# Token-major projections 512 columns wide, over two half slabs of weight rows, with four sums open

## The reference

```
h  = rms_norm(x);  p = h @ w_in            # q_a k_a v_a o_a i f q_b k_b v_b g_a g_b
y_a = sigmoid(o_a) * norm(mLSTM(silu(conv(q_a, k_a)), v_a, i, f))     # 8 heads
y_b = stick_breaking(norm(q_b), norm(k_b), v_b)                        # 8 heads
x  = x + (sigmoid(g_a) * y_a + sigmoid(g_b) * y_b) @ w_out
x  = x + square(relu(rms_norm(x) @ w_up)) @ w_down                     # 1024 -> 4096 -> 1024
h  = rms_norm(x);  p = h @ nsa_w_in        # q, 3 pairs of k and v, gates, z (3 x 1024)
o  = compressed, selected and window attention, 16 heads
y  = (sum over the three branches of gate * o * silu(z)) @ nsa_w_out
out = x + rms_norm(y)
```

## Time and profile before

| | |
|---|---|
| median of 3 runs | 1437.09 us |
| the profiled execution | 1437.17 us, its span 1435.4 us |
| mean granted TensorE clock | 0.994 of full speed |
| TensorE matmuls | busy 1393.7 us, 97% of the span |
| VectorE, ScalarE, GpSimd | busy 679.2, 612.0 and 173.8 us |
| DMA | 120.5 MB, mean 84 GB/s |

### The profile page before, as it was taken

One profiled execution on the slowest core, in us unless ns is written; L12 is line 12 of the kernel. 1 busy time (PEld: TensorE's weight loads), 2 busy tenths in 40 slices (PEclk: granted clock), 3 DMA queues, 4 the chain that ended last, 5 costly groups with the idle time before them and its releaser, 6 DMA issues.

```text
span 1435.4 us, 21763 instructions
## 1 busy us (share of the span) xinstructions
PE 1393.7 (97%) x9021; PEld 1219.5 (85%) x9021; DVE 679.2 (47%) x1152; ACT 612.0 (43%) x989; POOL 173.8 (12%) x243
## 2 busy tenths in 40 slices
PE   6999999999999999999999999999999999999998
PEld 4898777786777889899898998988899999898998
DVE  5653443553333453543434334341146777776654
ACT  4245444515555433421413214144424666665332
POOL 1001232001111000000000000000901333231000
PEclk9999999999999999999999999999999999999999
DMA  8655434343333333133222332244341322222221
GB/s 175 102 104 84 70 76 60 60 59 59 48 51 52 74 101 89 60 109 97 88 88 88 100 105 88 88 135 147 101 90 38 91 73 67 68 92 64 85 77 60
DMA packets 110559, 120.50 MB, mean 84 GB/s; under 512 B 5231, under 2 KB 106719, under 8 KB 110480
## 3 DMA queue, kind: packets, MB, share of 16 engines
q1 hardware_dynamic: 106960, 108.70, 31.4%
q0 software_dynamic: 3376, 10.38, 3.0%
q10 hardware_dynamic: 144, 0.31, 0.1%
HBM read 116.55 MB, written 2.82 MB: 83 GB/s over the span
## 4 chain that ended last, share of the span: by engine, by line
PE 87%; DVE 5%; ACT 2%; DMA 2%; issue 1%; POOL 1%; SPq 0%; DVEq 0%
PE ps_g L514 69%; PE ps_z L1107 2%; PE ps_z L1144 2%; PE ps_t L1179 2%; DMA w_raw<-in_w_in 2%; PE ps_z L985 1%; PE ps_z L973 1%; PE ps_t L961 1%; PE ps_t L908 1%; DVE w_lo L487 1%; PE ps_t L1029 1%; DVE probs L1653 1%; PE ps_z L896 1%; DMA tile_t<-bias_rev_dram 1%; PE ps_t L280 1%
## 5 line engine op out<-in xcount | busy, mean ns | idle before, releaser
L514 PE MATMUL ps_g<-act_hi,w_hi 128*128 128x512 f32 x784 | 309.8, 395 | 6.6 <-DVE act_lo L599 4.1
L487 DVE TENSOR_TENSOR w_lo<-w_raw,w_hi 128x2048 fp32r<-128x2048 f32 (+1 forms) x96 | 220.3, 2295 | 198.0 <-ACT w_hi L479 197.9
L514 PE MATMUL ps_g<-act_hi,w_lo 128*128 128x512 f32 x784 | 306.3, 391 | 0.0
L514 PE MATMUL ps_g<-act_lo,w_hi 128*128 128x512 f32 x784 | 305.9, 390 | 0.0
L479 ACT ACTIVATE w_hi<-w_raw 128x2048 fp32r<-128x2048 f32 (+1 forms) x96 | 182.0, 1896 | 178.0 <-PE ps_g L514 167.9
L514 PE MATMUL ps_g<-w_hi,act_hi 128*128 128x256 f32 x832 | 240.8, 289 | 1.4 <-DVE act_lo L597 0.7
L514 PE MATMUL ps_g<-w_lo,act_hi 128*128 128x256 f32 x832 | 235.1, 283 | 0.0
L514 PE MATMUL ps_g<-w_hi,act_lo 128*128 128x256 f32 x832 | 235.0, 282 | 0.0
L514 PEld LDWEIGHTS ps_g<-act_hi,w_hi 128*128 128x128 f32 x784 | 147.7, 188 | 39.4 <-DVE w_lo L487 4.5
L514 PEld LDWEIGHTS ps_g<-act_hi,w_lo 128*128 128x128 f32 x784 | 147.5, 188 | 31.5
L514 PEld LDWEIGHTS ps_g<-act_lo,w_hi 128*128 128x128 f32 x784 | 147.8, 188 | 29.7
(11 more groups left out here) (291 smaller groups left out, 1897.1 us busy)
## 6 DMA issues: line engine op xcount, KB each, us to landing
w_raw<-in_w_in SPq DMA_DIRECT2D x32, 1024.0 KB, 9.0
w_raw<-in_nsa_w_in SPq DMA_DIRECT2D x22, 1024.0 KB, 5.2
w_raw<-in_w_up SPq DMA_DIRECT2D x16, 1024.0 KB, 5.5
w_raw<-in_w_down SPq DMA_DIRECT2D x16, 1024.0 KB, 5.1
tile_t<-bias_rev_dram POOLq DMA_DIRECT2D x32, 256.0 KB, 3.2
w_raw<-in_w_out SPq DMA_DIRECT2D x4, 1024.0 KB, 5.1
w_raw<-in_nsa_w_out SPq DMA_DIRECT2D x4, 1024.0 KB, 5.2
x_sb<-in_x SPq DMA_DIRECT2D x4, 512.0 KB, 6.2
```

Source lines behind the costliest of these rows:

```text
L487: nc.vector.tensor_tensor(w_lo[b][:, :, 0:w], w_raw[b][:, :, 0:w], w_hi[b][:, :, 0:w].bitcast(F32), ALU.subtract).then_inc(lo_done, 1)
L514: mm = nc.tensor.matmul(o, stationary, moving, start=(k == 0 and j == 0), stop=(k == KT - 1 and j == 2))
```

## The change

Five groups of token-major slabs become wide: `va` (4 slabs), `wo` (4), `down` (16), the last 4 `nz` slabs (new kind `zw`) and `no` (4). Two neighbouring slabs of 1024 rows x 256 columns become two half slabs of 512 rows x 512 columns: as many slabs as before, of the same 1 MB. `mm_half` does 12 matmuls of 512 columns per token block and half slab. Four sums of 512 columns stay open from the first half slab to the second, in the 2 banks of `ps_g` and in banks 0 and 1 of `ps_z`; they are evacuated 512 columns wide during and after the second half. `vb`, `nvs`, `nvw` and the first 8 `nz` slabs stay as they are. The diff, cut to its core:

```diff
+WIDE = 512
+HALF_K = KT // 2
-        tile_free = [sem(f"tile_free{i}") for i in range(2)]
+        half_done = sem("half_done")
+        tile_free = [sem(f"tile_free{i}") for i in range(4)]
+        def add_wide(kind, mat, col0, n, row0=0):
+            first = len(slabs)
+            for i in range(n):
+                for half in range(2):
+                    slabs.append((mat, row0 + half * HALF_K * P, col0 + i * WIDE, WIDE, kind, i, half))
+            return first
-        N_VA = add("va", W, VA, 4)
+        N_VA = add_wide("va", W, VA, 2)
-        N_WO = add("wo", a["w_out"], 0, 4)
+        N_WO = add_wide("wo", a["w_out"], 0, 2)
-            add("down", a["w_down"], 0, 4, row0=quarter * D)
+            add_wide("down", a["w_down"], 0, 2, row0=quarter * D)
-        for z in (0, 1, 2, 4, 5, 6, 3, 7, 8, 9, 10, 11):
-            slabs.append((NW, 0, NZ + z * SLAB, SLAB, "nz", z))
-        N_NO = add("no", a["nsa_w_out"], 0, 4)
+        for z in (0, 1, 2, 4, 5, 6, 3, 7):
+            slabs.append((NW, 0, NZ + z * SLAB, SLAB, "nz", z, None))
+        N_ZW = add_wide("zw", NW, NZ + 8 * SLAB, 2)
+        N_NO = add_wide("no", a["nsa_w_out"], 0, 2)
...
+                for bank in (None, None, 2, 3) if slabs[n][4] == "no" else (2, 3, None, None):
+                    take(slabs[n][4], bank)
...
+        def bank(t):
+            g = bank_of[t]
+            return ps_g[:, g, :] if g < 2 else ps_z[:, (g - 2) * 512:(g - 1) * 512]
+        def wait_slab_used(eng, n, r=0):
+            if k_half(n) == 0:
+                eng.wait_ge(half_done, half_of[n] + 1 + MLP_HALVES * r)
+            else:
+                eng.wait_ge(tile_ready, tile_of[n + 1] + MLP_TILES * r)
...
+        def mm_half(pe, n, i, first_tile=None, hi=act_hi, lo=act_lo, r=0, activation_ready=None):
+            t, b, k0 = tile_of[n] + i, n % 2, k_half(n) * HALF_K
+            pe.wait_ge(lo_done, n + 1 + MLP_SLABS * r)
+            if k_half(n) == 0:
+                wait_bank(pe, t, r)
+            m = slice(i * P, (i + 1) * P)
+            wh, wl = slab_view(w_hi[b], n), slab_view(w_lo[b], n)
+            for k in range(k0, k0 + HALF_K):
+                if activation_ready is not None and i == 0:
+                    activation_ready(k)
+                if first_tile is not None and i == 0:
+                    wait_tile_free(pe, first_tile + k, r)
+                for j, (act, w) in enumerate(((hi, wh), (hi, wl), (lo, wh))):
+                    mm = nc.tensor.matmul(bank(t), act[:, k, m], w[:, k - k0, :], start=(k == 0 and j == 0),
+                                          stop=(k == KT - 1 and j == 2))
+            if k_half(n) == 1:
+                mm.then_inc(tile_ready, 1)
+            elif i == TB - 1:
+                mm.then_inc(half_done, 1)
...
-        def feature_tiles(pe, n, src, block_ready, between=None):
+        def feature_tiles(pe, n, src, block_ready, between=None, before=None):
...
+                if b == 0 and before is not None:
+                    wait_tile_free(pe, tile_of[before])
+                    wait_tile_free(pe, tile_of[before] + 1)
...
+            elif kind == "zw":                                      # act_evacuate
+                if i != 1:
+                    wait_tile_free(act, t - 2)
+                if i == 0:
+                    wait_tile_free(act, t - 1)
+                nc.scalar.activation(ev_t[:, g, :], bank(t), ACT.Tanh, scale=0.5).then_inc(ev_act, 1)
...
+            elif kind == "zw":                                      # dve_evacuate
+                after_act(dve, t, 1)
+                e = ev_t[:, g, :]
+                order.link(nc.vector.scalar_tensor_tensor(e, e, 1.0, ps, ALU.add, ALU.mult))
+                if s == 0:
+                    order.link(nc.vector.tensor_tensor(e, e, o_b[:, i, cols], ALU.mult))
+                else:
+                    nc.vector.tensor_tensor(e[:, 0:256], e[:, 0:256], o_b[:, i, 512:768], ALU.mult)
+                    order.link(nc.vector.tensor_tensor(e[:, 256:512], e[:, 256:512],
+                                                       o_w[i // 2][:, i % 2, :], ALU.mult))
+                nc.vector.tensor_tensor(o_a[:, i, cols], o_a[:, i, cols], e, ALU.add).then_inc(done, 1)
...
-            token_major = slabs[n][4] not in FEATURE                # dve_slab
+            token_major = slabs[n][4] not in FEATURE and k_half(n) is None
             if not token_major:
                 split_lo(dve, n + 1, r)
+            if k_half(n) == 0:
+                return
...
+                if n == N_VA:                                       # ScalarE, before the loop over tiles
+                    wait_tile_free(act, tile_of[N_IF])
+                    ... the gate rows' Abs, Exp and Ln, which stood between the tiles of slab N_VA
...
+                if h == 0:                                          # TensorE, first mLSTM head
+                    wait_tile_free(pe, tile_of[N_VA + 3])
+                    wait_tile_free(pe, tile_of[N_VA + 3] + 1)
...
                 else:                                               # TensorE, last attention unit
-                    mm_tile(pe, N_NZ + 8, 0)
+                    mm_half(pe, N_ZW, 0)
```

More of the change, by code:

```diff
@@ L606, in act_evacuate @@
             t = tile_of[n] + i
-            g, free = t % 2, tile_free[t % 2]
+            g, done = (bank_of[t] if k_half(n) is None else i) % 2, free(t)
             f = 2 * s + i
-            cols = slice(s * SLAB, (s + 1) * SLAB)
+            cols = slice(s * slabs[n][3], (s + 1) * slabs[n][3])
             if kind == "conv":
@@ L618, in act_evacuate @@
                 dst = v_a if kind == "va" else v_b
-                nc.scalar.copy(dst[:, i, cols], ps_g[:, g, 0:SLAB]).then_inc(free, 1)
+                nc.scalar.copy(dst[:, i, cols], bank(t)[:, 0:slabs[n][3]]).then_inc(done, 1)
             elif kind == "qb":
                 dst = q_b[:, f, :] if f < HB else k_b[:, f - HB, :]
-                nc.scalar.copy(dst, ps_g[:, g, :]).then_inc(free, 1)
+                nc.scalar.copy(dst, ps_g[:, g, :]).then_inc(done, 1)
             elif kind in ("oa", "ga"):
@@ L670, in dve_evacuate @@
             t = tile_of[n] + i
-            g, free = t % 2, tile_free[t % 2]
+            g, done = (bank_of[t] if k_half(n) is None else i) % 2, free(t)
             f = 2 * s + i
-            cols = slice(s * SLAB, (s + 1) * SLAB)
-            ps = ps_g[:, g, :]
+            cols = slice(s * slabs[n][3], (s + 1) * slabs[n][3])
+            ps = bank(t)
             if kind == "conv":
@@ L687, in dve_evacuate @@
                         order.link(ins)
-                ins.then_inc(free, 1)
+                ins.then_inc(done, 1)
             elif kind == "if":
@@ L1225, in _ @@
                     split_hi(act, n + 1)
-                for i in range(tiles_of(n)):
+                if n == N_VA:
+                    wait_tile_free(act, tile_of[N_IF])
+                    order.link(nc.scalar.activation(rows[0][:], rows[2][:], ACT.Abs))
+                    order.link(nc.scalar.activation(rows[0][:], rows[0][:], ACT.Exp, scale=-1.0))
+                    nc.scalar.activation(rows[0][:], rows[0][:], ACT.Ln, bias=1.0).then_inc(gate_act, 1)
+                for i in range(0 if k_half(n) == 0 else tiles_of(n)):
                     if n == N_IF - 1 and i == 1:
@@ L1229, in _ @@
                     act_evacuate(act, n, i)
-                    if n == N_VA and i == 1:
-                        wait_tile_free(act, tile_of[N_IF])
-                        order.link(nc.scalar.activation(rows[0][:], rows[2][:], ACT.Abs))
-                        order.link(nc.scalar.activation(rows[0][:], rows[0][:], ACT.Exp, scale=-1.0))
-                    if n == N_VA and i == 3:
-                        nc.scalar.activation(rows[0][:], rows[0][:], ACT.Ln, bias=1.0).then_inc(gate_act, 1)
                 if n == N_VA + 1:
@@ L1712, in _ @@
             dve.wait_ge(s_out, 32)
-            for n in range(N_NZ + 8, N_NO):
+            for n in range(N_ZW, N_NO):
                 dve_slab(dve, order, n)
```

164 lines of the change are left out of this document (100 added, 64 removed).

## The result

The changed kernel takes 1412.55 us (median), the kernel before, run beside it, 1437.28 us: 24.7 us less. The ratio is 0.9827, with a 95% interval of 0.9808 to 0.9846. The forecast was 1413.6 us. The profiled execution took 1412.27 us (span 1410.4), against 1437.17 (span 1435.4). One run of 3517.78 us, whose cause no profile shows, is counted in that median but not in the ratio; the median of the other three (1411.71 to 1412.84) is 1412.27 us.

What follows compares the result with a forecast made beforehand. TensorE was taken to bound the kernel, busy 1393.7 of 1435.4 us, mostly with projection matmuls. From 1437.17 us, -20.1 (pace) - 5.7 (waits that go) + 2.3 (waits that come) = -23.5 gave 1413.6 us, range 1409 to 1419.

Steps and rivals of the forecast that it cites:

- The pace (-20.1): Token-major stages: 1536 wide matmuls at 0.2269 us replace 3072 narrow at 0.1200, saving 0.0131 each, 20.1 us.
- whatever its width: Projection matmuls: each carries a fixed 0.0131 us beside its column cost, at any number of columns.
- The waits that go (-5.7): `wo`, `down`, last `nz` slabs, `no`: later-needed input blocks and an unpaced first `no` tile save 3.0, 1.0 and 1.7 us.
- `down` stop: `down` stages: idle on the last block's `up_lo`, 1.1 us over four, plus 0.16 for each stop, would go.
- The waits that come (+2.3): Norms, `zw` to `no` and tail: wider last evacuations add 0.8, 0.9 and 0.6 us.
- `zw` to `no`: Before `no`: TensorE waits for the release of the last `o_a` tile's bank, its next step about 0.9 us later.
- The tail's sum: After the last matmul: square +0.22, product +0.27, array +0.11; 3.8 us instead of 3.2 to the output step's end.
- the table load in the first tile is caught up: Last slab: VectorE's loop of about 2.6 us per tile, against TensorE's 2.72, makes up the table load's delay.
- rival C: Growing pauses (`zw` to `no`, norms) drop the clock; 24 `no` matmuls at half clock cost 5.4 us: 1419.0 us; chance 0.07.
- A: Token-major stages: a wide matmul costs exactly two narrow, 0.2400; only the waits' 3.4 us saved: 1433.7 us; chance 0.06.
- B: Token-major stages: fixed part mostly not tied to matmul count, about a fifth saved: 1429.7 us; chance 0.03.
- D: Wide stages: changing banks among four open sums starves TensorE and drops its clock, slower than before: 1472 us; chance 0.04.

Runs made afterwards that it cites:

- e1: Changed kernel with every wide matmul of 512 columns issued as two of 256 into the same bank: 1431.21 us, ratio to before 0.9971.
- e2: Changed kernel with every wide matmul issued as four of 128 columns: 1766.30 us in the profiled run.
- e4: Changed kernel, but the first tile of `wo` and `down` waits for all eight row blocks of its input: 1438.56 us, ratio to before 1.0022.
- e3: Changed kernel, but in first half slabs of `va` and `down` TensorE changes its open sum every 3 matmuls: 1418.06 us, ratio to before 0.9882.
- e9: Changed kernel with the first matmul of the first `wo` tile issued four times instead of once: 1413.83 us, a single profiled execution.
- e8: Changed kernel with only the last half slab of `wo` and of each `down` issued as two matmuls of 256 columns: 1417.92 us, one profiled execution.

## Why the prediction was right

**The pace (-20.1).** Right. The nearest row, with the roles of the operands exchanged, gave 0.2269; measured 0.2266. Against e1 the term is 13.3 ns per wide matmul, 20.4 us over 1536. The Trainium skill, "TensorE: Matmul & The Clock Gate", section "Wait — 56ns, not 53.3ns?", has about 2.5 ns over the columns; e1 against the changed kernel shows five times that for this float32 stream. What was wrong in this step is "whatever its width": e2's 128 columns cost 0.112, where the step's sum gives 0.067. The forecast did not use that width.

**The waits that go (-5.7).** Right. No matmul of `wo` or `down` waits for `y_lo` or `up_lo` in the changed kernel. The price of a `down` stop was a little low: its stage took 46.60 us before and 46.07 in e1, where the stop is gone, so 0.53 instead of 0.44. That the first tile asks for only half of its input is worth keeping: in e4, waiting for the other four blocks too costs 14.8 us idle and more in clock. The first tile of `no` is no longer paced. Its first matmul and the first of the next tile in TensorE's timeline, 12 matmuls apart:

```profile
1360.11 0.47 PE L600 MATMUL ps_g<-w_hi,act_hi 128*128 128x512 f32 x1 [0.74 <-DVE act_lo L691]
...
1362.93 0.39 PE L600 MATMUL ps_g<-w_hi,act_hi 128*128 128x512 f32 x1
```

2.82 for 12 instead of the 2.72 of the stream, where the earlier trace rows show 4.55 for 2.88.

**The waits that come (+2.3).** `zw` to `no`: forecast +0.9, measured 0.85 (5.25 us from the first transpose of `o_a` to `no`, against 4.40 before, from 1377.10 to the 1381.50 of the earlier trace rows). The wait is the one that was named, the release of the last tile of `o_a`, seen in TensorE's timeline:

```profile
1357.95 0.77 PE L628 MATMUL ps_g<-cst,o_a 128*128 128x128 f32 x5 [0.64 <-DVE o_a L844]
```

The pauses ahead of both norms grew as forecast, from the last matmul to the first transpose 2.48 against 2.10 us. The tail's sum was right (3.83 against 3.84) by a path that was not: "the table load in the first tile is caught up" is wrong, since in the chain above VectorE still goes from one output step straight to the next product.

**What was missed.** The clock behind the norms. The earlier trace rows showed that it fell before; the prediction let it fall again and priced the transposes at no change. In the profile it stayed at 1.00, worth 1.5 + 1.4 us, the opposite of rival C; why is not shown. Against this stands the slower start, -2.7 us of chance. Their sum is near zero, so that the forecast's error of 1.1 us is smaller than either: that it is so small is luck. Taken without both, the measured saving is 25.0 - 2.9 + 2.7 = 24.8 us against 23.5; 0.8 of the rest is in the MLP: four stops at 0.53 instead of 0.44 (0.4 us), and 768 wide matmuls that saved 0.0134 instead of 0.0131 (0.2 us; 2 x 0.1200 in e1's window less 0.2266).

**The rivals.** A and B fell with the pace. C did not come about: `no` ran at 1.00 from its first matmul (window above), and so did the transposes in both profiles of the changed kernel. It was luck in part, since in e3 and e9, with the same pauses, the clock fell behind one norm. D fell with the windows of `down` and `no` and with e3. On D the Trainium skill's section "A second HAM failure mode: psum-queue depth-cycling" on the same page warns of idle moments of TensorE when it cycles through banks at 512 columns; with four open sums, and in e3 with a change every three matmuls, the granted clock is 1.00 throughout these streams, and the only stops in them are e3's four on `up_lo`.

## What to carry to other kernels

Where TensorE is full, read the step from one matmul's start to the next at two widths before changing anything: twice the narrow step less the wide one, times the count, was 20 of this change's 25 us, and it carried over to exchanged operands within 0.3 ns. Halve the depth of a stage's first tile where you can: with half the row blocks asked for later, no stop was left in `wo` and `down`, and asking for all of them at once cost the whole gain. And do not price a pause by its idle time alone: behind those of 1.8 to 3.7 us the clock may or may not fall, which was worth another 1.3 to 1.7 us each time.

## What was not expected of the hardware

- A matmul of 128 columns (0.112 us) costs nearly what one of 256 does (0.120), and one of 512 costs 0.227, each with a stationary block of its own, at granted clock 1.00.
- The longer pause (2.09 us after wide matmuls) kept clock 1.00 in 12 of 14 cases (12 of 16 with e4), the shorter (1.83 us after narrow ones) lost it in 4 of 4, and 2.10 us after narrow ones (e1, e2, e8) in 6 of 6.
- Behind the same pause of 2.9 us in the same code the clock fell to 0.50 in 9 of 13 profiles and stayed at 1.00 in 4; the work from there to the next projection tile took 5.2 us in the changed kernel's profile and 3.5 in e9.
